# Seven block products for eight in the down-projections and half of the first output projection

## The chip, the cores and the metric

The kernel runs on one core of a Trainium2 chip. The metric is the device time of one execution in microseconds (us). Five engines run their own instruction streams in order: TensorE (PE; its weight loads, PEld, overlap its matmuls), VectorE (DVE), ScalarE (ACT), GpSimd (POOL) and SyncE (SP), which here only issues DMAs. They wait for each other by semaphores.

## What is computed

Two transformer blocks on 256 tokens of width 2048, all in fp32. The first has stick-breaking attention with 16 heads and an MLP with squared ReLU, the second has a mixer of chunked attention and windowed means and a gated MLP with a causal convolution of width 3. Cut to the matrix products that matter here:

```python
# first block
h = x + stick_breaking_mixer(rms_norm(x, norm_mix), w_qkv, w_o)   # ... @ w_o: 2048 x 2048
h = h + jnp.square(relu(rms_norm(h, norm_mlp) @ mlp_w1)) @ mlp_w2 # 2048 x 8192, 8192 x 2048
x = rms_norm(h, final_norm)
# second block
m = concat([attention(q, k, v), pooled], -1) @ w_o_2
x = x + rms_norm(m, post_mix_g)
up = causal_dwconv(rms_norm(x, pre_ffn_g) @ w_up, conv_w, conv_b) # 2048 x 11264
y = (gelu(up[..., :5632]) * up[..., 5632:]) @ w_down              # 5632 x 2048
x = x + rms_norm(y, post_ffn_g)
```

## The kernel before, in words

**Pieces.** Every weight matrix is cut into strips of 512 columns, and a strip into pieces of 256 rows. A piece is one DMA of 512 KB into one of six slots of `raw` (128 partitions, 2 row tiles of 512). `plan_program` writes all 746 pieces and everything around them into one list of steps; each engine's program walks the list and emits what concerns it, so the list is each engine's order. There is no scheduler.

**Three products for one.** An fp32 number is carried as two rounded halves, hi and lo. ACT copies `raw` to `Wh` (L986), DVE makes `Wl = raw - Wh` (L1204), and TensorE computes hi x Wh, hi x Wl and lo x Wh. The tokens are the stationary side, in halves of 128. A piece is 2 token halves x 2 row tiles x 3 = 12 matmuls of 128x512 into the two PSUM banks of one set (`row_products`, all at L1546). Two sets, 0 and 1, take turns from strip to strip; the four banks of set 2 are for side work (scores, turning tiles).

**How far ahead.** `Wh` and `Wl` have `NW = 5` slots. The split of piece i+4 stands in the list just ahead of the products of piece i, and ACT may write it once piece i-1 has been multiplied. So ACT and DVE are never more than four pieces ahead of TensorE. A load of SP waits until the piece six loads earlier has been split.

**Side work around the pieces.** It is put into the same list at a given distance in pieces. Where a strip of `mlp_w1` or `w_up_2` ends, ACT moves the result from PSUM to `T0` (`stage_rows`, L1042 or L1044), SP sends it to DRAM and, three pieces later, reads it back in another order (`land_rows`, L917), and four more pieces later DVE turns 32x32 blocks (`turn_strip`, L1256). For `mlp_w1`, ACT and DVE then split it into `hid1` (L1084, L1325). For `w_up_2`, ACT makes the newest tap of the convolution (L1125, four instructions), DVE the older taps (L1416, eight instructions), ACT the gelu (L1129), POOL the gating product (L1529, 5.5 us), and ACT and DVE split that into `hid2` (L1133, L1422). The row results of `w_o`, `mlp_w2` and `w_down_2` are added on DVE (L1286, L1283, L1440; the first sums of `w_down_2` are copied, L1427), squared and summed on ACT (L998), multiplied by gains on DVE in the last round of the MLP (L1292), and moved over DRAM and turned for the next product (`move_rows` L901 and L906, `turn_blocks` L1296, L1004, L1300).

**The strip pairs.** Output strips of `w_o`, `mlp_w2` and `w_down_2` come in pairs (`strip_pair`). The MLP runs in three rounds (24, 20 and 20 hidden tiles of 128): some strips of `mlp_w1`, then the pair of output columns 0 to 1023, then the pair of 1024 to 2047, over that round's hidden tiles. The gated MLP does the same in two rounds (24 and 20 tiles). I call the two pairs of a round the opening and the second pair.

Of the kernel before, what the change touches and what calls it, by code (L numbers as in the profile page):

```python
# [10 lines left out]
KT = 16  # L11
# [3 lines left out]
NW = 5  # L15
# [37 lines left out]
def plan_program(sem):  # L53
    p = Plan(sem)
    step, done, after, later = p.step, p.done, p.after, p.later
    free = {n: [] for n in ("QK1", "T0", "T1", "E", "zs", "set0", "set1", "set2", "mT", "qk0", "qk1", "v0", "v1", "A0", "A1")}
    st = {}
    now = [0]

    def side_set():  # L60
        return 2
# [60 lines left out]

    def row_squares(n, need, gained=False):
# [6 lines left out]
    def row_norm(squared=False, into=None):  # L130
# [156 lines left out]
    def values(g, blk):  # L287
        def f():
# [4 lines left out]
            free[f"set{s}"] = [lo]  # L293
            oHL_tiles[4 * g:4 * g + 4] = [lo] * 4
# [44 lines left out]
    for s4 in (0, 2):  # L339
        strip_pair("sb_w_o", s4, ALL8, 0 if s4 else 2, "oHL1", oHL_tiles, [evac_rows(s4, "mlp"), evac_rows(s4 + 1, "mlp")])  # L340
# [1445 lines left out]
```

## Time and profile before

| | |
|---|---|
| median of 3 runs | 2097.33 us (2096.52 to 2098.95) |
| profiled execution, its time | 2095.49 us |
| its span (first to last instruction) | 2093.8 us |
| PE busy | 2083.5 us, 9304 matmuls |
| DVE busy | 1224.2 us |
| ACT busy | 1072.2 us |
| granted TensorE clock, mean | 0.999 |
| DMA | 469 MB, mean 224 GB/s |

Start with the busy shares, then ask of each engine what ended its idle time. The share of DVE and ACT is a mean over the program; how far ahead of TensorE they are has to be read place by place in the order of time.

### The profile page before, as it was taken

What the parts mean: (1) busy time and instruction counts of PE and PEld (TensorE: products, weight loads), DVE (VectorE), ACT (ScalarE), POOL (GpSimd) and SP (SyncE); (2) the same over time, 40 slices, a digit from 0 to 9 for tenths busy, and PEclk for the clock granted to TensorE, in tenths of its full rate; (3) what the DMA queues carried; (4) which work ended last, traced back from release to release, by engine and by line L of the source; (5) the groups of instructions that cost most, each with busy time, mean ns of one, the idle gap of its engine ahead of it and who ended that gap; (6) DMA issues with size and microseconds to landing.
All of it is one profiled execution on the core that took longest, in us unless ns stands there. A gap on an engine that the chain in (4) does not pass through costs nothing.

```text
span 2093.8 us, 23749 instructions
## 1 busy us (share of the span) xinstructions
PE 2083.5 (100%) x9304; PEld 1728.1 (83%) x9304; DVE 1224.2 (58%) x1312; ACT 1072.2 (51%) x1303; POOL 119.7 (6%) x66
## 2 busy tenths in 40 slices
PE   9999999999999999999999999999999999999998
PEld 8888888888888888888888888888888888888887
DVE  6546556655554555455566755566666654566665
ACT  7555654555434543455455554455555533555553
POOL 3000000000000000000002000000112100011120
PEclk9999999999999999999999999999999999999999
DMA  8688666888667885688588777667878766787863
GB/s 297 197 251 236 191 188 216 260 248 235 211 193 206 241 254 194 196 243 238 192 270 232 229 244 232 197 203 211 249 236 250 220 211 193 223 247 242 251 221 121
DMA packets 291903, 469.46 MB, mean 224 GB/s; under 512 B 18512, under 2 KB 82128, under 8 KB 291280
## 3 DMA queue, kind: packets, MB, share of 16 engines
q1 hardware_dynamic: 290928, 463.46, 72.5%
q10 hardware_dynamic: 864, 4.49, 0.6%
q8 instruction: 73, 1.20, 0.2%
q14 instruction: 38, 0.31, 0.0%
HBM read 432.75 MB, written 35.13 MB: 223 GB/s over the span
## 4 chain that ended last, share of the span: by engine, by line
PE 96%; DVE 1%; DMA 1%; ACT 1%; issue 0%; SPq 0%; ACTq 0%; DVEq 0%
PE ps L1546 96%; DMA T<-passed_strip 1%; DVE Wl L1204 0%; DVE zs L1416 0%; ACT Wh L986 0%; DMA E<-passed_rows 0%; DVE T L1256 0%; DMA gains<-in_gains_dram 0%; DVE E L1416 0%; ACT zs L1125 0%; SPq L917 0%; DMA passed_rows<-xN 0%; ACT T L1044 0%; DVE aHL L1307 0%; PE ps L1549 0%
## 5 line engine op out<-in xcount | busy, mean ns | idle before, releaser
L1204 DVE TENSOR_TENSOR Wl<-raw,Wh 128x1024 fp32r<-128x1024 f32 x743 | 908.2, 1242 | 674.2 <-ACT Wh L986 673.6
L1546 PE MATMUL ps<-Wh,aHL 128*128 128x512 f32 x3712 | 1148.8, 390 | 2.4 <-DVE Wl L1204 0.8
L986 ACT ACTIVATE Wh<-raw 128x1024 fp32r<-128x1024 f32 x743 | 768.0, 1054 | 611.1 <-PE ps L1546 608.7
L1546 PEld LDWEIGHTS ps<-Wh,aHL 128*128 128x128 f32 x3712 | 696.8, 188 | 147.9 <-DVE Wl L1204 1.3
L1546 PE MATMUL ps<-Wl,aHL 128*128 128x512 f32 x1856 | 722.1, 389 | 0.0
L1546 PE MATMUL ps<-Wh,hid 128*128 128x512 f32 x1728 | 532.8, 389 | 0.0
L1546 PEld LDWEIGHTS ps<-Wl,aHL 128*128 128x128 f32 x1856 | 348.4, 188 | 71.8
L1546 PEld LDWEIGHTS ps<-Wh,hid 128*128 128x128 f32 x1728 | 324.3, 188 | 67.4
L1546 PE MATMUL ps<-Wl,hid 128*128 128x512 f32 x864 | 336.1, 389 | 0.0
L1546 PEld LDWEIGHTS ps<-Wl,hid 128*128 128x128 f32 x864 | 162.2, 188 | 33.7
L1546 PE MATMUL ps<-Wh,oHL 128*128 128x512 f32 x512 | 159.0, 390 | 0.0
L1546 PEld LDWEIGHTS ps<-Wh,oHL 128*128 128x128 f32 x512 | 96.1, 188 | 20.0
L1529 POOL TENSOR_TENSOR E<-E,zs 128x1024 f32<-128x1024 f32 x11 | 60.9, 5534 | 794.8 <-DVE E L1416 794.8
L1546 PE MATMUL ps<-Wl,oHL 128*128 128x512 f32 x256 | 99.6, 389 | 0.0
L1256 DVE STREAM_TRANSPOSE T<-T 128x1024 f32<-128x1024 f32 x38 | 47.2, 1242 | 17.1 <-DMA T<-passed_strip 17.1
L1546 PEld LDWEIGHTS ps<-Wl,oHL 128*128 128x128 f32 x256 | 48.1, 188 | 9.8
L1044 ACT ACTIVATE T<-ps,rs 128x512 f32<-128x512 f32 x72 | 46.0, 676 | 15.6 <-PE ps L1546 7.9
L1520 POOL TENSOR_TENSOR QK<-E 128x1020 f32<-128x1020 f32 x2 | 3.8, 1886 | 821.6 <-DVE E L1256 821.6
L1125 ACT ACTIVATE E<-T,conv 128x256 f32<-128x256 f32 x44 | 22.9, 590 | 44.5 <-DVE T L1256 44.5
L1133 ACT ACTIVATE hid<-E 128x1024 fp32r<-128x1024 f32 x11 | 11.7, 1061 | 65.6 <-POOL E L1529 65.6
L1125 ACT ACTIVATE zs<-T,conv 128x256 f32<-128x256 f32 x44 | 22.9, 590 | 31.9 <-DVE T L1256 31.9
L1084 ACT ACTIVATE hid<-T 128x1024 fp32r<-128x1024 f32 x16 | 17.0, 1062 | 39.2 <-DVE T L1256 39.2
(167 smaller groups left out, 687.4 us busy)
## 6 DMA issues: line engine op xcount, KB each, us to landing
raw<-in_mlp_w_dram SPq DMA_DIRECT2D x256, 512.0 KB, 4.5
raw<-in_w_up_dram SPq DMA_DIRECT2D x176, 512.0 KB, 4.6
raw<-in_sb_w_qkv_dram SPq DMA_DIRECT2D x93, 512.0 KB, 5.2
raw<-in_w_down_dram SPq DMA_DIRECT2D x88, 512.0 KB, 4.7
raw<-in_w_in_dram SPq DMA_DIRECT2D x64, 512.0 KB, 4.8
passed_strip<-T SPq DMA_DIRECT2D x104, 256.0 KB, 4.5
T<-passed_strip SPq DMA_DIRECT2D x208, 128.0 KB, 5.2
raw<-in_sb_w_o_dram SPq DMA_DIRECT2D x32, 512.0 KB, 5.4
```

The lines of the kernel that those rows point to most:

```text
L986: e.activation(Wh[:, i % NW, :], rawv[:, i % NRAW, :], ACT.Copy).then_inc(st["hi"][0], 1)
L1044: e.activation(strip_rows[:, t, :], ps[st["set"]][:, t, :], ACT.Copy, scale=cols[st["col"]][:, t:t + 1]).then_inc(st["staged"][t][0], 1)
L1084: e.activation(hid1[:, st["t0"]:st["t0"] + 4, 0:TOK], T1[:, :, :], ACT.Copy).then_inc(st["hi"][0], 1)
L1125: e.activation(C[:, m, :], T1[:, m, :], ACT.Identity, scale=conv[:, 2, n0 + m:n0 + m + 1], bias=conv[:, 3, n0 + m:n0 + m + 1]).then_inc(st ...
L1133: e.activation(hid2[:, st["t0"]:st["t0"] + 4, 0:TOK], E4, ACT.Copy).then_inc(st["hi"][0], 1)
L1204: e.tensor_tensor(Wl[:, i % NW, :], rawv[:, i % NRAW, :], Wh[:, i % NW, :].bitcast(F32), ALU.subtract).then_inc(st["lo"][0], 1)
L1256: e.transpose(dst, strip_blocks).then_inc(st["done"][0], 1)
L1520: e.tensor_tensor(dst[:, a:4, sh:TOK], src[:, a:4, sh:TOK], src[:, a:4, 0:TOK - sh], ALU.add).then_inc(added[0], 1)
L1529: e.tensor_tensor(E4, E4, Z4, ALU.mult).then_inc(st["done"][0], 1)
L1546: return e.matmul(o, l, r, start=start, stop=stop, skip_group_check=True)
```

## The change

A group of two neighbouring strips x one row pair x two token halves is a 2x2 block product: A (tokens) in four 128x128 blocks, B (weights) in four 128x512 blocks. It takes eight block products of three matmuls before, and seven after, in Winograd's form of Strassen's scheme. 32 groups are done so: two in the second pair of `w_o`, and the first three of each of the ten pairs of `mlp_w2` and `w_down_2`.

- Two pieces become four, s0 to s3, of 6, 6, 6 and 3 matmuls (`seven_products`). s0 and s1 are loaded; the weights of s2, s3 and half of s1 are sums, made by DVE in four additions of 128x512 (`weight_sums`), of which one is in place in `raw`. Each of the four takes a slot of `Wh` and `Wl`, and seven halves of 512 columns are split where four were. `NW` stays 5, and the distances in the list are still counted in pieces.
- The sums of token blocks are made once for each row pair: four DVE instructions, one ACT and one DVE to split them (`mix_tokens`), put behind the hidden tiles or values that they need.
- Four of the seven products collect in the banks of set 2, the others in sets 0 and 1. After the third group (in `w_o` the second), ACT copies one bank and DVE adds the banks into the output rows in eight instructions of 128x512 (`fold`; five in the first round of `w_down_2`, which initialise them).
- In a pair the order is two plain pieces, group, two plain pieces, group, and so on, then the rest. The second strip's PSUM set is now taken by the first group, after two pieces, and not after all plain pieces of the first strip.
- The RMS factor of the MLP is applied under the ReLU (ACT, `scale=`) and no longer squared at the sums, whose scalar_tensor_tensor becomes tensor_tensor; `y_first` adds where it copied.

```diff
+        b[0]["first"], b[0]["start"] = False, (False, True)
+        rest = a[2:n] + b[:n]
+        p.pieces[first:] = a[:2]
+        for m, kp in enumerate(sevens):
+            seven(w, s4, kp, mov, tiles, (a[0]["strip"], b[0]["strip"]), koff, m, m == 0, fold if m == len(sevens) - 1 else None)
+            p.pieces += rest[2 * m:2 * m + 2] if m < len(sevens) - 1 else rest[2 * m:]
+        p.pieces += a[n:] + b[n:]
...
+    def seven(w, s4, kp, mov, tiles, pair, koff, m, opens, fold):
+
+        for i, kind in enumerate(("s0", "s1", "s2", "s3")):
+            src = (w, "rows", kp * 256, (s4 + i) * STRIP) if i < 2 else None
...
+                if t0 < 8:
+                    free["E"] = [lo, mix_tokens("hid2", "E", t0 // 2, 2 if t0 == 0 else 1, [g])]
...
+        if n == 0:
+            made = {m: done("weights_added") for m in (1, 3, 2, 4)}
+            step("weight_sums", a=raw_of[i] % NRAW, b=raw_of[i + 1] % NRAW, need=[landed(i), landed(i + 1), *free["sums"]], made=made)
...
+        step("split", i=i, part=q["kind"], slot=raw_of.get(i, 0) % NRAW, loaded=landed(i) if n == 0 else q["made"],
+             used=(mm_sem, i - NW + 1), hi=(hi_sem, i + 1), lo=(lo_sem, i + 1))
...
+        elif q["kind"] == "s0":
+            if q["opens"]:
+                now[0] = 1 - now[0]
+                set_of[q["pair"][1]] = now[0]
+                need += free[f"set{now[0]}"] + free["set2"]
...
+                elif k == "weight_sums":
...
+                    e.tensor_tensor(wsum[:, 0, :], a[:, 0, :], b[:, 0, :], ALU.add).then_inc(made[1][0], 1)
+                    e.tensor_tensor(b[:, 0, :], b[:, 0, :], b[:, 1, :], ALU.add).then_inc(made[3][0], 1)
+                    e.wait_ge(*made[1])
+                    e.tensor_tensor(wsum[:, 1, :], wsum[:, 0, :], b[:, 1, :], ALU.add).then_inc(made[2][0], 1)
+                    e.wait_ge(*made[2])
+                    e.tensor_tensor(wsum[:, 2, :], wsum[:, 1, :], a[:, 1, :], ALU.add).then_inc(made[4][0], 1)
...
+                elif k == "fold":
...
+                    e.wait_ge(*st["copied"])
+                    e.tensor_tensor(wsum[:, 0, :], P[:, 0, :], wsum[:, 0, :], ALU.add).then_inc(m[0][0], 1)
...
+                    e.tensor_tensor(x[:, 0, a], x[:, 0, a], P[:, 0, :], ALU.add).then_inc(m[1][0], 1)
+                    e.wait_ge(*m[0])
+                    e.tensor_tensor(wsum[:, 1, :], P[:, 2, :], wsum[:, 0, :], ALU.add).then_inc(m[2][0], 1)
+                    e.tensor_tensor(wsum[:, 2, :], P[:, 1, :], wsum[:, 0, :], ALU.subtract).then_inc(m[3][0], 1)
+                    e.wait_ge(*m[2])
+                    e.tensor_tensor(x[:, 1, a], x[:, 1, a], wsum[:, 1, :], ALU.add).then_inc(m[4][0], 1)
+                    e.wait_ge(*m[3])
+                    e.tensor_tensor(wsum[:, 0, :], P[:, 1, :], wsum[:, 1, :], ALU.subtract).then_inc(m[5][0], 1)
+                    e.tensor_tensor(x[:, 0, b], x[:, 0, b], wsum[:, 2, :], ALU.add).then_inc(m[6][0], 1)
+                    e.wait_ge(*m[5])
+                    e.tensor_tensor(x[:, 1, b], x[:, 1, b], wsum[:, 0, :], ALU.add).then_inc(m[7][0], 1)
...
+            def seven_products(q):
...
+                terms = {"s0": (("a11", side[:, 0, :], q["opens"], True), ("a12", a[:, 0, :], False, False)),
+                         "s1": (("d1", side[:, 2, :], q["opens"], True), ("d3", b[:, 0, :], q["opens"], False)),
+                         "s2": (("d0", side[:, 1, :], q["opens"], True), ("d2", side[:, 3, :], q["opens"], True)),
+                         "s3": (("a22", a[:, 1, :], False, False),)}[q["kind"]]
```

**Place 1: DVE in the opening pair of `w_down_2`, first round.** `T1<-T0` is the turning of a strip, `zs` and `E` are the two operands of the gate (128x255 and 128x254 are the older taps), `hid2` is the split of the gated tiles, `Wl` that of a weight piece. Before:

```order
L1204 TENSOR_TENSOR Wl<-raw,Wh 128x1024 [waits s_w_hi] x7
L1256 STREAM_TRANSPOSE T1<-T0 128x1024 [waits s_conv_newest,s_conv_older,s_strip_moved]
L1204 TENSOR_TENSOR Wl<-raw,Wh 128x1024 [waits s_w_hi]
L1416 SCALAR_TENSOR_TENSOR E<-T1,conv,E 128x255 [waits s_conv_newest] x2
L1416 SCALAR_TENSOR_TENSOR E<-T1,conv,E 128x254 [waits s_conv_older] x2
...
L1204 TENSOR_TENSOR Wl<-raw,Wh 128x1024 [waits s_w_hi] x3
L1422 TENSOR_TENSOR hid2<-E,hid2 128x4x256 [waits s_hid_hi]
```

After; `wsum` holds the sums of weights:

```order
L1328 TENSOR_TENSOR Wl<-wsum,Wh 128x1024 [waits s_w_hi]
L1328 TENSOR_TENSOR Wl<-wsum,Wh 128x512 [waits s_w_hi]
L1328 TENSOR_TENSOR Wl<-raw,Wh 128x1024 [waits s_w_hi] x2
L1334 TENSOR_TENSOR wsum<-raw 128x512 [waits s_w_lo,s_raw3,s_raw2]
L1335 TENSOR_TENSOR raw<-raw 128x512
L1337 TENSOR_TENSOR wsum<-wsum,raw 128x512 [waits s_weights_added]
L1339 TENSOR_TENSOR wsum<-wsum,raw 128x512 [waits s_weights_added]
L1328 TENSOR_TENSOR Wl<-raw,Wh 128x1024 [waits s_w_hi] x2
L1328 TENSOR_TENSOR Wl<-wsum,Wh 128x1024 [waits s_w_hi]
L1431 STREAM_TRANSPOSE T1<-T0 128x1024 [waits s_conv_newest,s_conv_older,s_strip_moved]
L1328 TENSOR_TENSOR Wl<-wsum,Wh 128x512 [waits s_w_hi]
```

From the older taps of one strip to the turning of the next stood seven splits for 84 matmuls. Now seven splits for 51 matmuls stand there (s2, s3, two plain pieces, s0, s1, s2: 6 + 3 + 24 + 18), with four additions among them, and behind the turning waits the split of s3, of 3 matmuls.

**Place 2: DVE in the second pair of the last round of `mlp_w2`.** `T1<-E` turns result rows for the next product, `aHL` is their low half. Before:

```order
L1296 STREAM_TRANSPOSE T1<-E 128x1024 [waits s_hid_lo,s_rows_moved]
L1300 SCALAR_TENSOR_TENSOR aHL<-T1,gains,aHL 128x256 [waits s_tile_hi] x4
L1204 TENSOR_TENSOR Wl<-raw,Wh 128x1024 [waits s_w_hi] x4
L1296 STREAM_TRANSPOSE T1<-E 128x1024 [waits s_tile_lo,s_rows_moved]
L1300 SCALAR_TENSOR_TENSOR aHL<-T1,gains,aHL 128x256 [waits s_tile_hi] x4
L1204 TENSOR_TENSOR Wl<-raw,Wh 128x1024 [waits s_w_hi] x3
```

After:

```order
L1467 STREAM_TRANSPOSE T1<-E 128x1024 [waits s_hid_lo,s_rows_moved]
L1471 SCALAR_TENSOR_TENSOR aHL<-T1,gains,aHL 128x256 [waits s_tile_hi] x4
L1328 TENSOR_TENSOR Wl<-raw,Wh 128x1024 [waits s_w_hi]
L1334 TENSOR_TENSOR wsum<-raw 128x512 [waits s_w_lo,s_raw5,s_raw4]
L1335 TENSOR_TENSOR raw<-raw 128x512
L1337 TENSOR_TENSOR wsum<-wsum,raw 128x512 [waits s_weights_added]
L1339 TENSOR_TENSOR wsum<-wsum,raw 128x512 [waits s_weights_added]
L1328 TENSOR_TENSOR Wl<-raw,Wh 128x1024 [waits s_w_hi] x2
L1328 TENSOR_TENSOR Wl<-wsum,Wh 128x1024 [waits s_w_hi]
L1467 STREAM_TRANSPOSE T1<-E 128x1024 [waits s_tile_lo,s_rows_moved]
L1471 SCALAR_TENSOR_TENSOR aHL<-T1,gains,aHL 128x256 [waits s_tile_hi] x4
L1328 TENSOR_TENSOR Wl<-wsum,Wh 128x512 [waits s_w_hi]
```

Between the two turnings stood four splits for 48 matmuls; now there are four splits for 30 (12 + 6 + 6 + 6) and four additions.

## Rows read from the trace of the kernel before

**Rows 1.** The page: span, and busy us of each engine with its share

```profile
span 2093.8 us, 23749 instructions
...
PE 2083.5 (100%) x9304; PEld 1728.1 (83%) x9304; DVE 1224.2 (58%) x1312; ACT 1072.2 (51%) x1303; POOL 119.7 (6%) x66
```

**Rows 2.** TensorE's waits: us in total, times, longest us

```profile
PE ps L1546 <- ACT zs L1149: 2.3, 1, 2.3
```

**Rows 3.** Windows: length, PE, PEld, DVE, ACT, POOL busy (x), granted clock, DMA share, GB/s

```profile
500.00:700.00 200.00, 200.00 (x884) 165.62 (x883) 101.89 (x88) 86.36 (x89) 0.00 (x0) 1.00 0.70 212
2086.00:2093.00 7.00, 1.41 (x3) 0.30 (x2) 3.77 (x10) 1.93 (x5) 0.00 (x0) 0.83 0.51 185
```

**Rows 4.** The timeline of TensorE from 600 us: start us, us, what

```profile
600.41 0.62 PE L1546 MATMUL ps<-Wh,hid 128*128 128x512 f32 x2
...
601.09 0.62 PE L1546 MATMUL ps<-Wh,hid 128*128 128x512 f32 x2
```

**Rows 5.** The timeline of DVE in a plain stretch; idle time before, and its releaser

```profile
529.23 1.23 DVE L1204 TENSOR_TENSOR Wl<-raw,Wh 128x1024 fp32r<-128x1024 f32 x1 [1.50 <-ACT Wh L986]
```

**Rows 6.** Groups by line: busy us, mean ns of one, idle before

```profile
L1204 DVE TENSOR_TENSOR Wl<-raw,Wh 128x1024 fp32r<-128x1024 f32 x743 | 908.2, 1242 | 674.2 <-ACT Wh L986 673.6
...
L1286 DVE TENSOR_TENSOR xN<-xN,ps 128x512 f32<-128x512 f32 x8 | 5.1, 681 | 0.0
...
L986 ACT ACTIVATE Wh<-raw 128x1024 fp32r<-128x1024 f32 x743 | 768.0, 1054 | 611.1 <-PE ps L1546 608.7 <-DMA raw<-in_sb_w_qkv_dram 2.0
```

**Rows 7.** The timeline of DVE, opening pair of w_down_2, first round

```profile
1620.98 1.22 DVE L1422 TENSOR_TENSOR hid<-E,hid 128x1024 fp32r<-128x1024 f32 x1 [3.38 <-ACT hid L1133]
1622.12 4.62 DVE L1204 TENSOR_TENSOR Wl<-raw,Wh 128x1024 fp32r<-128x1024 f32 x4
1626.66 1.24 DVE L1256 STREAM_TRANSPOSE T<-T 128x1024 f32<-128x1024 f32 x1
1630.99 1.23 DVE L1204 TENSOR_TENSOR Wl<-raw,Wh 128x1024 fp32r<-128x1024 f32 x1 [3.09 <-ACT Wh L986]
1632.13 3.25 DVE L1416 SCALAR_TENSOR_TENSOR zs<-T,conv,zs 128x255 f32<-128x255 f32 x8
...
1650.06 1.25 DVE L1256 STREAM_TRANSPOSE T<-T 128x1024 f32<-128x1024 f32 x1 [2.86 <-DMA T<-passed_strip]
1654.41 1.22 DVE L1204 TENSOR_TENSOR Wl<-raw,Wh 128x1024 fp32r<-128x1024 f32 x1 [3.10 <-ACT Wh L986]
```

**Rows 8.** The timeline of ACT there

```profile
1627.93 2.08 ACT L1125 ACTIVATE zs<-T,conv 128x256 f32<-128x256 f32 x4 [3.20 <-DVE T L1256]
1629.91 1.04 ACT L986 ACTIVATE Wh<-raw 128x1024 fp32r<-128x1024 f32 x1
1630.86 1.24 ACT L1044 ACTIVATE T<-ps,rs 128x512 f32<-128x512 f32 x2
```

**Rows 9.** The timeline of SP there: the strip's way back from DRAM

```profile
1640.26 1.97 SPq L917 DMA_DIRECT2D T<-passed_strip  x4
```

**Rows 10.** Matmuls on hidden tiles after 1500 us: ns min/median/max, first and last start

```profile
L1546 PE MATMUL ps<-Wh,hid x704: 389/389/389, 1628.3 to 2085.0; 128*128 128x512 f32 x176
```

**Rows 11.** The timeline of DVE, second round's opening pair

```profile
1968.41 3.49 DVE L1204 TENSOR_TENSOR Wl<-raw,Wh 128x1024 fp32r<-128x1024 f32 x3
...
1973.76 1.25 DVE L1256 STREAM_TRANSPOSE T<-T 128x1024 f32<-128x1024 f32 x1 [0.16 <-DMA T<-passed_strip]
```

**Rows 12.** The timeline of DVE around the last round's second pair of mlp_w2

```profile
1019.97 1.40 DVE L1283 SCALAR_TENSOR_TENSOR xN<-ps,rs,xN 128x512 f32<-128x512 f32 x2
...
1038.19 1.24 DVE L1296 STREAM_TRANSPOSE T<-E 128x1024 f32<-128x1024 f32 x1
1040.01 1.69 DVE L1300 SCALAR_TENSOR_TENSOR aHL<-T,gains,aHL 128x256 fp32r<-128x256 f32 x4 [0.58 <-ACT aHL L1004]
...
1049.51 1.25 DVE L1296 STREAM_TRANSPOSE T<-E 128x1024 f32<-128x1024 f32 x1 [2.72 <-DMA E<-passed_rows]
```

**Rows 13.** The timeline of DVE at the second turning in w_o's pairs

```profile
358.94 1.25 DVE L1296 STREAM_TRANSPOSE T<-E 128x1024 f32<-128x1024 f32 x1 [2.57 <-DMA E<-passed_rows]
```

More of the change, by code:

```diff
@@ L55, in plan_program @@
     step, done, after, later = p.step, p.done, p.after, p.later
-    free = {n: [] for n in ("QK1", "T0", "T1", "E", "zs", "set0", "set1", "set2", "mT", "qk0", "qk1", "v0", "v1", "A0", "A1")}
+    free = {n: [] for n in ("QK1", "T0", "T1", "E", "zs", "set0", "set1", "set2", "mT", "qk0", "qk1", "v0", "v1", "A0", "A1", "sums")}
     st = {}
     now = [0]
+    taken = []
     def side_set():
+        assert not taken
         return 2
@@ L90, in strip, with strip_pair @@
             p.pieces.append(dict(src=src, shape=2, mov=mov, kt=2 * (kp - koff), tiles=tiles, kind="N", first=n == 0,
-                                 last=n == len(ks) - 1, evac=evac, early=None, strip=strips[0]))
+                                 start=(n == 0, n == 0), last=n == len(ks) - 1, evac=evac, early=None, strip=strips[0]))
         return first
-    def strip_pair(w, s4, ks, tail, mov, tiles, evacs, koff=0):
-        first, n = len(p.pieces), len(ks) - tail
+    def strip_pair(w, s4, ks, tail, mov, tiles, evacs, koff=0, sevens=(), fold=None):
+        plain = [kp for kp in ks if kp not in sevens]
+        first, n = len(p.pieces), len(plain) - tail
@@ new lines, in strip_pair @@
+        b[0]["first"], b[0]["start"] = False, (False, True)
[5 more added lines that the diff above has]
+        p.pieces += a[n:] + b[n:]
+        order = [q["strip"] if q["kind"] == "N" else 0 for q in p.pieces[first:]]
@@ new lines, in strip_pair @@
+        assert max(j for j, k in enumerate(order) if k == 0) < max(j for j, k in enumerate(order) if k == a[0]["strip"])
+        assert min(j for j, k in enumerate(order) if k == 0) < min(j for j, k in enumerate(order) if k == b[0]["strip"])
+        return first
+    def seven(w, s4, kp, mov, tiles, pair, koff, m, opens, fold):
+        for i, kind in enumerate(("s0", "s1", "s2", "s3")):
+            src = (w, "rows", kp * 256, (s4 + i) * STRIP) if i < 2 else None
+            p.pieces.append(dict(src=src, shape=2, mov=mov, kt=2 * (kp - koff), tiles=tiles, kind=kind, m=m, first=False,
+                                 opens=opens, last=False, evac=None, early=None, strip=None, pair=pair,
+                                 fold=fold if i == 3 else None, closes=fold is not None))
@@ L293, in f @@
             free[f"set{s}"] = [lo]
+            if blk == 1 and g == 0:
+                free[f"set{s}"] = [lo, mix_tokens("oHL1", "values", 0, 2, [lo])]
             oHL_tiles[4 * g:4 * g + 4] = [lo] * 4
@@ L617, in f @@
                 d = [done("y_kept") for t in range(2)]
-                step("y_first", s4=s4, set=s, mm=k, done=d)
+                step("y_first", s4=s4, set=s, mm=k, folded=st.pop(("fold", s4)), done=d)
                 free[f"set{s}"] = [d[1]]
@@ L681, in split @@
             load_x_rest(i)
-            load(i + NRAW)
+            load(raw_of[i] + NRAW)
+        elif i < N and p.pieces[i]["kind"][0] == "s":
+            sums_and_split(i)
         elif i < N:
-            step("split", i=i, loaded=(raw[i % NRAW], 16 * (i // NRAW + 1)), used=(mm_sem, i - NW + 1) if i >= NW else None,
+            step("split", i=i, part="N", slot=raw_of[i] % NRAW, loaded=landed(i), used=(mm_sem, i - NW + 1) if i >= NW else None,
                  hi=(hi_sem, i + 1), lo=(lo_sem, i + 1))
             load_x_rest(i)
-            load(i + NRAW)
+            load(raw_of[i] + NRAW)
     x_rows = []
@@ L741, in plan_program @@
                 need.append(tok)
-        q["set"], q["n"] = 2 if q["kind"] == "P" else set_of[q["strip"]], i
+        q["n"] = i
+        q["set"] = 2 if q["kind"] == "P" else [set_of[n] for n in q["pair"]] if q["kind"][0] == "s" else set_of[q["strip"]]
         if i < N - HELD:
@@ L759, in plan_program @@
             q["evac"](q["set"], k)
+        if q.get("fold"):
+            taken.clear()
+            q["fold"](q["set"], k)
         for job in p.later_steps.pop(i, ()):
```

209 lines of the change are left out of this document (160 added, 49 removed).

## The prediction

> **What bounds the kernel now.** The page first: PE is busy in 2083.5 of 2093.8 us, DVE in 58% and ACT in 51% [rows 1]. Then PE's own waits, to see whether it ever stands: the longest is 2.3 us, at the very end [rows 2]. So TensorE sets the time and each matmul taken away is worth its pitch. The timeline of TensorE gives it: three matmuls, one block product, start every 601.09 - 600.41 = 0.68 us [rows 4], at a granted clock of 1.00, which is the 2.4 GHz level, in the window of 500 to 700 us [rows 3]. A plain piece lasts 2.72 us.
>
> The second thing to see is by how much the splits are early, since the change takes from exactly this. In a plain stretch DVE waits 1.50 us for ACT ahead of each split [rows 5]: a piece's slot is free when TensorE begins the piece four places earlier, ACT's hi takes 1.05 us, DVE's lo 1.23, and with the waits the piece is ready about 2.6 us after that start, 10.9 - 2.6 = 8.3 us early. This lead is the cover of everything DVE and ACT do besides.
>
> **What is taken away.** 32 groups x one block product = 96 matmuls: 32 x 0.68 = **21.8 us**. All on the path.
>
> **What is added, in a stretch where nothing else happens.** A group and the two plain pieces behind it: TensorE 7 x 0.68 + 5.44 = 10.2 us. DVE: five splits of 1024 at 1.14 us (four in a row took 4.62 from start to end, the last one's tail included [rows 7]), half a split, 0.65, and four additions of 512. A 512-wide tensor_tensor takes 0.68 and, back to back, 5.1/8 = 0.64 [rows 6]; one addition waits for the one before it, so 2.6 for four. Sum 8.95 of 10.2 us. ACT needs 5.5 x 1.05 = 5.8. So the scheme holds by itself, but only by 1.25 us in 10.2, and the lead is smaller: four places ahead are now s1, s2, s3 and a plain piece, say, and not 48 matmuls. Worked through place by place, s0 is ready some 2.7 us ahead of its use, and a plain piece behind s3 some 2.4 us. Anything above 2.5 us that DVE has to do, or to wait for, inside the groups makes TensorE stand. The fold (8 additions, about 5.4 us, once per pair) does not: four plain pieces, 10.9 us, are split ahead of it, and the next split is ready about 1 us early. The tokens' sums in the strips of `mlp_w1` cost DVE and ACT about 4 us against the full lead: nothing. The new scale under the ReLU and the changed row sums: within 0.1 us each, nothing.
>
> On 512-wide additions the Trainium skill (VectorE: DVE Perf Modes, The TRN2 errata) says that each instruction pays a fixed time, and gives an fp32 tensor_tensor (N+151)/0.96 ns. That makes 0.69 us for 512; the trace agrees, 0.68 alone [rows 6], but back to back the fixed part is mostly hidden (0.64 and 1.14), so four additions priced by the page would be 2.8 and not 2.6 us.
>
> **Opening pair of w_down_2, first round** (place 1 of the change). The pair's first matmul starts at 1628.3 [rows 10]. With unchanged times up to there, s0 is due at 1628.3 + 5.4 = 1633.7, s1 at 1635.1, s2 at 1636.4, s3 at 1637.8. DVE: the four splits from 1622.12 become three, to 1625.5 [rows 7]; additions to 1628.3; lo of s0 to 1629.5; the turning, 1.24, to 1630.7; ACT's four taps of 2.08 in all [rows 8] to 1632.8; ACT's hi of s1 to 1633.9, then the two copies to `T0`, 1.24 together, to 1635.1, which free the PSUM set that the group now needs at once (due 1633.7), hi of s2 to 1636.1. DVE: lo of s1 to 1635.1, eight older taps, 3.2 [rows 7], to 1638.2, lo of s2 to 1639.4. TensorE stands about 3 us by then, and 0.6 more for the plain piece behind s3, since ACT's gelu stands ahead of its hi. The next strip's way back from DRAM: SP issues it behind a load that waits for that plain piece's split, at 1642.1; in the trace the turning starts 9.8 us after the issue at 1640.26, having waited for it [rows 7, 9]; so 1651.9. Before that, DVE has the splits up to the next group's s2 ready, and s3 is due at 1651.6. But turning 1.25, taps on ACT 2.1, hi and lo of s3 1.3: 1656.5, **4.9 us late**. Then 3.2 of older taps and the split of a plain piece, due 0.7 after s3 began: **3.6 us late**. Last, the gate's split (POOL 5.6 us, then ACT and DVE, which waits: 3.38 us before [rows 7]) stands between s0 and s1 of the third group: 1.0. Sum **13 us**. Before, the same block, 9.8 us from the turning to the end of the second split, met about 8 us of pieces already split and 2.7 us of the one between.
>
> **Second round's opening pair.** The same order, DVE a little earlier against TensorE: three splits are done at 1971.9 [rows 11], 4.6 us ahead of the pair's start, and not 2.8. That spares 2.5 of the first 3.6 us: **10 us**.
>
> **Second pair of the last MLP round** (place 2). DVE adds rows, ACT squares them, DVE multiplies them by gains, ACT squares again, each ahead of a split; one turning with its four low halves takes 1038.19 to 1041.7, 3.5 us, and a split follows 0.5 later [rows 12]. Against TensorE, with the pair's times from 1020.2: s3 of the first group is ready 16.6 after that and due at 15.0 (1.6 late), the plain pieces behind it 0.8 and, behind the turning, 2.5 late, s0 of the next group 1.1; the second turning waits for its rows until about 30 (before: to 1049.51, with a wait of 2.72 [rows 12]), so the s3 behind it is 3 late. Sum **9.5 us**.
>
> **Second pair of w_o.** The same without gains and squares: 0.6 behind the first turning; the second waits for its rows (2.57 before [rows 13]), and s2 and s1's lead are used up: 5. Sum **5.5 us**.
>
> **The rest.** Opening pairs of `mlp_w2`: a turning, ACT's and DVE's halves, 3.6 us, between s2 and s3 against a lead of 2.9 and 0.4 behind it: 1 us each, 3. The tokens' sums of `hid2` stand behind the gate's split, where the lead had already shrunk to about 2.2 us (the split that starts at 1622.12 is due at 1625.6 [rows 7, 10]): 4.1 and 2.6 us of work, 2.3 us per round, 4.6. The sums of `oHL1` the same way, 0 to 2, taken as 1. The other six second pairs and the program's end: nothing.
>
> Sum of the stalls: 13 + 10 + 9.5 + 5.5 + 3 + 4.6 + 1 = **46.6 us** against 21.8. On the profiled execution (2095.5 us) that is +24.8, 2120.3; the median lies 1.8 us above it, so **2122 us**. From below the stalls are bounded by what waits for nothing outside DVE and ACT: the block of turning, taps and hi and lo alone, without DRAM's delay, by a rough estimate 60% of the sum, 28 us; from above by DMA landings later by 1 to 2 us at six turnings, 60 us.
>
> **Rivals.**
> - *The lead is better than I make it, and TensorE hardly stands.* For it: means of 58% and 51% [rows 1]; DVE would rise only to about 69%. DVE's idle time in front of ACT is large. Against it: the row-by-row order above. It needs all stalls under 17 us. At 10 us of stalls: 2097.3 - 21.8 + 10 = 2086 us. This one ends faster; it decides at the turning between s2 and s3, if that costs under 2 us and not 8.5. Chance 0.14.
> - *Stalls and saving about cancel*: DVE's backlog is eaten by its own idle gaps, 17 to 28 us of stalls: 2093 to 2103, middle 2098. Chance 0.14.
> - *The clock falls in the stalls.* In the trace's last 7 us, where TensorE stood 2.3 us and more, the granted clock was 0.83 in the mean, between 1.2 and 2.4 GHz [rows 2, 3]; nowhere before had it stood as long. Some five stalls here are of 3.5 to 5 us. If each brings the clock down and one plain piece after it runs at half rate, that is 5 x 2.7 = 13.5 us more, 2136. Against it: after most of the stalls DVE is the later one, and slower matmuls hide in its time. Chance 0.12. The Trainium skill (TensorE: Matmul & The Clock Gate, HAM oscillation) states this rule, that a TensorE standing too long restarts at half clock; no row here shows it in the middle of a kernel.
> - *The forecast*, 2103 to 2133. Chance 0.60.
>
> **The numbers.** Low end 2090 (leaves out most of the first rival), high end 2138 (takes in the clock). Faster and slower are counted from 0.2%, 4.2 us, about what a measurement of this kernel can tell. Faster: the first rival, 0.14. Same, 2093 to 2101.5: half of the second and a little, 0.08. Slower: 0.78.
>
> **What would show it.** In the profile after: 9208 matmuls and a pitch of still 0.68 per three; PE's waits on DVE's splits of 40 to 50 us in all, where before they were 0.8; the longest of 4 to 5 us at the s3 behind a turning in both opening pairs of `w_down_2`; DVE near 69%; the plain strips as long as before. Wrong: if PE's waits on DVE stay under 15 us, the lead was misjudged; if the pitch of the group's matmuls is not 0.227 us each, the saving was.

## The result, and the profile after

The changed kernel takes **2136.18 us** (median of 4 runs, 2134.44 to 2138.98), against 2096.93 (2095.73 to 2098.95) for the kernel before beside it: a ratio of 1.0187, 95% interval 1.0170 to 1.0205. It is slower by 39 us where I forecast 25. The profiled execution took 2138.98 us, the most of the four; so the stages below, read from the profiles, account for 43 us and not for 39. Its page, busy us and share of each engine [rows 1]:

```profile
span 2136.7 us, 24135 instructions
...
PE 2086.4 (98%) x9208; PEld 1718.6 (80%) x9208; DVE 1428.4 (67%) x1640; ACT 1136.3 (53%) x1390; POOL 121.9 (6%) x66
```

There are 96 matmuls fewer, as there should be, and PE is busy for 2.9 us longer: part of them ran slowly, as shown below. TensorE's waits [rows 2]; columns: us in total, times, longest:

```profile
PE ps L1719 <- DVE Wl L1328: 31.9, 23, 3.3
PE ps L1719 <- ACT T L1167: 3.7, 2, 2.6
PE ps L1722 <- DVE xN L1463: 3.4, 1, 3.4
PE ps L1719 <- DVE aHL L1471: 2.6, 1, 2.6
```

The first line is the splits. The second is the PSUM set that a group needs at once and that ACT still has to copy. The third and fourth are no weights at all: rows of the next stage's input that come late.

To see where the time went I measured each stage from the start of its first matmul to that of the next stage's (the last row: to the start of the last matmul on weights). Us, from the starts in both traces; "forecast" is the time before, less the saving, plus the prediction's stalls:

| stage | before | forecast | after |
|---|---|---|---|
| `w_o`, second pair | 43.5 | 47.6 | 45.9 |
| `mlp_w1`, first round | 130.6 | 130.6 | **135.0** |
| three opening pairs of `mlp_w2` | 174.1 | 171.0 | 170.6 |
| second pairs of `mlp_w2`, rounds 1 and 2, and of `w_down_2`, round 1 | 185.0 | 178.9 | 178.8 |
| second pair of `mlp_w2`, round 3 | 54.4 | 61.9 | 61.6 |
| `w_in_2` | 188.4 | 188.4 | **193.6** |
| `w_up_2`, both rounds | 483.0 | 487.6 | **494.3** |
| opening pair of `w_down_2`, round 1 | 65.3 | 76.2 | 76.5 |
| the same, round 2 | 54.4 | 62.4 | 64.4 |
| second pair of `w_down_2`, round 2 | 54.2 | 52.1 | **54.3** |

The pairs themselves came out nearly as worked through in their sums. For the profiled execution I forecast 2120.3 us, 18.7 too few. 16.3 of them lie in other stages, in bold; with the last pair's 2.2 nearly all are found.

**The opening pair of `w_down_2`**, DVE in the first round [rows 7]; start us, us, engine, line, op, tiles, idle time before and its releaser:

```profile
1649.99 1.24 DVE L1431 STREAM_TRANSPOSE T<-T 128x1024 f32<-128x1024 f32 x1
1654.32 1.23 DVE L1328 TENSOR_TENSOR Wl<-raw,Wh 128x1024 fp32r<-128x1024 f32 x1 [3.09 <-ACT Wh L1100]
1655.46 3.24 DVE L1587 SCALAR_TENSOR_TENSOR zs<-T,conv,zs 128x255 f32<-128x255 f32 x8
...
1668.37 1.22 DVE L1328 TENSOR_TENSOR Wl<-wsum,Wh 128x1024 fp32r<-128x1024 f32 x1
1669.54 1.25 DVE L1431 STREAM_TRANSPOSE T<-T 128x1024 f32<-128x1024 f32 x1
1673.44 0.69 DVE L1328 TENSOR_TENSOR Wl<-wsum,Wh 128x512 fp32r<-128x512 f32 x1 [2.66 <-ACT Wh L1100]
1674.05 3.24 DVE L1587 SCALAR_TENSOR_TENSOR E<-T,conv,E 128x255 f32<-128x255 f32 x8
1677.21 2.36 DVE L1328 TENSOR_TENSOR Wl<-raw,Wh 128x1024 fp32r<-128x1024 f32 x2
```

The second turning starts behind a split and finds its rows there, the split of s3 comes 3.9 us later, then the older taps, then the plain piece. SP had issued the rows' way back [rows 9] here:

```profile
1662.97 1.95 SPq L1025 DMA_DIRECT2D T<-passed_strip  x4
```

TensorE there [rows 4]:

```profile
1674.19 0.50 PE L1719 MATMUL ps<-Wh,hid 128*128 128x512 f32 x1 [1.80 <-DVE Wl L1328]
1674.53 0.40 PE L1719 MATMUL ps<-Wl,hid 128*128 128x512 f32 x1
1674.76 0.40 PE L1719 MATMUL ps<-Wh,hid 128*128 128x512 f32 x1
1678.48 0.80 PE L1719 MATMUL ps<-Wh,hid 128*128 128x512 f32 x1 [3.32 <-DVE Wl L1328]
1679.08 0.63 PE L1719 MATMUL ps<-Wl,hid 128*128 128x512 f32 x1
1679.50 1.05 PE L1719 MATMUL ps<-Wh,hid 128*128 128x512 f32 x2
```

Three matmuls of s3, and TensorE stands for 3.32 us. Then it goes on at half its rate: 1679.08 to 1679.50 is 0.42 us from start to start, where 0.23 was normal. Windows of these moments [rows 3]; length, PE, PEld, DVE, ACT, POOL busy, granted clock, DMA share, GB/s:

```profile
1647.30:1688.00 40.70, 32.63 (x123) 25.01 (x122) 34.07 (x45) 21.34 (x29) 6.24 (x1) 0.87 0.55 172
400.00:412.00 12.00, 9.40 (x35) 7.32 (x34) 7.04 (x14) 7.12 (x11) 0.00 (x0) 0.86 0.69 218
1460.00:1472.00 12.00, 9.93 (x37) 7.77 (x36) 8.44 (x10) 6.23 (x8) 0.00 (x0) 0.86 0.65 186
```

By such starts there are eight slow stretches of four matmuls or more, 67 matmuls in all with 13.9 us more than at the full rate; before there was none. DVE is busy in 34.1 of the pair's first 40.7 us, and waits for ACT in most of the rest.

**The first strips of `mlp_w1`** show a stall that I had not looked for. DVE adds the result rows of `w_o`'s second pair (L1457) and turns them (L1467); before, the same are L1286 and L1296. Before:

```profile
365.19 1.28 DVE L1286 TENSOR_TENSOR xN<-xN,ps 128x512 f32<-128x512 f32 x2
...
384.18 1.28 DVE L1286 TENSOR_TENSOR xN<-xN,ps 128x512 f32<-128x512 f32 x2
...
396.20 1.25 DVE L1296 STREAM_TRANSPOSE T<-E 128x1024 f32<-128x1024 f32 x1 [4.47 <-DMA E<-passed_rows]
```

After:

```profile
375.17 1.28 DVE L1457 TENSOR_TENSOR xN<-xN,ps 128x512 f32<-128x512 f32 x2
...
386.18 1.25 DVE L1467 STREAM_TRANSPOSE T<-E 128x1024 f32<-128x1024 f32 x1 [3.28 <-DMA E<-passed_rows]
...
392.44 1.28 DVE L1457 TENSOR_TENSOR xN<-xN,ps 128x512 f32<-128x512 f32 x2
...
403.32 1.25 DVE L1467 STREAM_TRANSPOSE T<-E 128x1024 f32<-128x1024 f32 x1 [4.29 <-DMA E<-passed_rows]
```

The pair starts at 340.2 before and 341.2 after, `mlp_w1` at 383.7 and 387.0. The groups stand among the pieces of the pair's *first* strip, so that its rows are added 34.0 us after the pair's start and not 25.0. Its turning then falls just ahead of the second strip's rows: these are added 5.4 us after `mlp_w1` began, and not 0.5, and turned 16.3 us after, not 12.5. TensorE is there first:

```profile
406.13 0.67 PE L1719 MATMUL ps<-Wh,aHL 128*128 128x512 f32 x1 [2.60 <-DVE aHL L1471]
```

**`w_up_2`**: DVE where the first tokens' sums of `hid2` stand:

```profile
1460.89 1.23 DVE L1593 TENSOR_TENSOR hid<-E,hid 128x1024 fp32r<-128x1024 f32 x1 [3.38 <-ACT hid L1256]
...
1463.16 0.42 DVE L1354 TENSOR_TENSOR wsum<-wsum,E 128x256 f32<-128x256 f32 x1
1464.71 1.22 DVE L1356 TENSOR_TENSOR hidMix<-wsum,hidMix 128x1024 fp32r<-128x1024 f32 x1 [1.13 <-ACT hidMix L1108]
1465.85 3.49 DVE L1328 TENSOR_TENSOR Wl<-raw,Wh 128x1024 fp32r<-128x1024 f32 x3
```

From the end of the gate's split, 1462.1, to the start of the next weight's at 1465.85 are 3.7 us, and TensorE stood for 2.1 us until 1467.2. The second sums, 46 us later, take only 2.7 us and made it stand for 2.2.

### The profile page after: what moved, and what is told of

Its sections match the earlier page's. It is cut to its first block and busy times, and to the rows that moved or that the text cites. A ratio compares the mean times of both kernels' runs of the same rounds, so it can differ in the third digit from the quotient of the medians.

```text
span 2136.7 us, 24135 instructions
## 1 busy us (share of the span) xinstructions
PE 2086.4 (98%) x9208; PEld 1718.6 (80%) x9208; DVE 1428.4 (67%) x1640; ACT 1136.3 (53%) x1390; POOL 121.9 (6%) x66
## 5 line engine op out<-in xcount | busy, mean ns | idle before, releaser
L1719 PE MATMUL ps<-Wh,hid 128*128 128x512 f32 x1428 | 455.3, 395 | 23.7 <-DVE Wl L1328 19.9
L1719 PEld LDWEIGHTS ps<-Wh,hid 128*128 128x128 f32 x1428 | 271.6, 190 | 88.3 <-DVE Wl L1328 27.2
L1719 PE MATMUL ps<-Wl,hid 128*128 128x512 f32 x714 | 280.8, 393 | 0.0
L1719 PEld LDWEIGHTS ps<-Wl,hid 128*128 128x128 f32 x714 | 135.9, 190 | 27.9
L1719 PE MATMUL ps<-Wh,hidMix 128*128 128x512 f32 x240 | 79.5, 392 | 1.4 <-DVE Wl L1328 1.4
L1328 DVE TENSOR_TENSOR Wl<-wsum,Wh 128x1024 fp32r<-128x1024 f32 x64 | 60.1, 963 | 21.7 <-ACT Wh L1100 21.6
L1100 ACT ACTIVATE Wh<-wsum 128x1024 fp32r<-128x1024 f32 x64 | 52.2, 834 | 13.8 <-PE ps L1719 13.8
L1719 PEld LDWEIGHTS ps<-Wh,hidMix 128*128 128x128 f32 x240 | 45.3, 189 | 11.9 <-DVE Wl L1328 2.4
```

Source lines behind the costliest of these rows:

```text
L1100: e.activation(Wh[:, i % NW, c], src, ACT.Copy).then_inc(st["hi"][0], 1)
L1328: e.tensor_tensor(Wl[:, i % NW, c], src, Wh[:, i % NW, c].bitcast(F32), ALU.subtract).then_inc(st["lo"][0], 1)
L1719: return e.matmul(o, l, r, start=start, stop=stop, skip_group_check=True)
```

## The experiments

Times are compared with the kernel before on the same chip (2094.9 to 2095.5 us there). The edits are given in short form; the kernels name the pairs that have groups in one table. A stage's time is that of the one profiled execution.

**The crowded places plain.**

```diff
-                   sevens=(0, 1) if s4 else (), fold=fold_into("xN", s4, lambda: [x_rows[-1]]))
+                   sevens=(), fold=fold_into("xN", s4, lambda: [x_rows[-1]]))
...
-                           sevens=tuple(range(2 * at, 2 * at + 3)), fold=...
+                           sevens=() if c == 2 and s4 == 2 else tuple(...), fold=...    # mlp_w2
+                           sevens=() if s4 == 0 else tuple(...), fold=...               # w_down_2
```

> The changed kernel without the groups of seven at the four places where a turning stands among them: second pair of w_o, last second pair of mlp_w2, both opening pairs of w_down_2 (21 of 32 groups stay; all token sums are still made). Theory, the lead is used up only there: the two w_down_2 pairs come back from 76.5 and 64.4 us to 65.3 and 54.4, the mlp_w2 pair from 61.6 to 54.4, the w_o pair from 45.9 to 43.5, and the starts of mlp_w1 and w_in_2 behind two of them (4.4 and 5.2 us longer) as well; in all about 40 us less, 2096. Rival, the load of DVE as such makes TensorE stand, wherever it is: a third less of it brings a third of the lost time back, 2120 or so.

Measured: 2101.33 us (2096.64 to 2105.23, 10 runs), ratio 1.0025 [1.0016, 1.0035]: the theory, some 5 us above its number. `mlp_w1` took 131.1 us, `w_in_2` 188.4 and the last round's second pair of `mlp_w2` 54.9. So 35 of the 41 us hang on 11 of the 32 groups, and what `mlp_w1` and `w_in_2` take longer goes with the groups in the pair ahead of them. What stays lies mostly in `w_up_2` (+5.2 and +3.8) and in the openings, which were 1.6 and 2.9 above before without a group of their own.

**Weight sums of two columns.**

```diff
-    e.tensor_tensor(wsum[:, 0, :], a[:, 0, :], b[:, 0, :], ALU.add)
+    e.tensor_tensor(wsum[:, 0, 0:2], a[:, 0, 0:2], b[:, 0, 0:2], ALU.add)   # and so the other three
```

> The changed kernel with the four additions of each weight sum cut from 512 columns to 2, all waits kept; the products of the sums are not the right ones. It takes some 1.8 us of DVE out of each group, 58 us in all. Theory (place and lead, a chain of turning, ACT and split): opening pairs of w_down_2 stay over 70 and 59 us, since the chain behind the turning stays; in all 2112 to 2122. Rival (DVE's load): every pair comes down to two us under its old time, in all 2085 to 2095.

The other 510 columns of each sum hold old values. Measured: 2137.11 us, one run. Neither theory gives this time, and only the openings are as the first said. DVE was busy for 61.5 us less (1366.9, 64% of the span), and TensorE waited for its splits as long as before, 32.1 us. The openings of `w_down_2` fell by 2.8 and 3.3 us, to 73.7 and 61.1, for some 5 us of DVE's time spared in each; the opening pair of `mlp_w2` in round 2 rose by 4.0, to 58.2, `mlp_w1` in the first round to 136.4, `w_in_2` to 195.3. DVE's mean load is not what holds TensorE up; what the losses elsewhere came from is open.

**Later.** Tokens' sums of `hid2` eight pieces later in both rounds, and ten plain pieces ahead of the first group in the first round's opening of `w_down_2`; the second round's opening keeps its order.

```diff
-    p.pieces[first:] = a[:2]
+    p.pieces[first:] = (a[:n] + b[:n])[:at]          # at = 10 in that pair, 2 in all others
...
-    free["E"] = [lo, mix_tokens("hid2", "E", t0 // 2, 2 if t0 == 0 else 1, [g])]
+    later(8, mix)                                     # the same call
```

> Two edits at two places. In the first round's opening pair of w_down_2 the first group comes after ten plain pieces and not after two, the same work in another order; and the token sums of hid2 are made eight pieces later, in both rounds. Theory: that pair goes from 76.5 us to 64 or 66; w_up_2 strips from 272.0 and 222.3 to 267 and 219; in all 2136 - 11 - 8 = 2117. Rival (DVE's load): the same instructions, so the same time, 2136 give or take 3.

Measured: 2122.33 us (2117.61 to 2124.10, 4 runs), ratio 1.0131 [1.0114, 1.0148]. The profiled execution is the fastest of the four, 2117.61. The rival falls; of the theory, the strips of `w_up_2` did better than said and are back at exactly 265.4 and 217.6 us, but the first round's opening took 69.4 and not 64 to 66, with three stalls of 2.3, 2.5 and 0.9 us left in it. The second round's took 62.3, 2.1 less, though its groups were not moved. DVE in `w_up_2`, with the gate's split at the same place as above and no sums behind it:

```profile
1460.97 1.23 DVE L1600 TENSOR_TENSOR hid<-E,hid 128x1024 fp32r<-128x1024 f32 x1 [3.37 <-ACT hid L1263]
1462.11 3.49 DVE L1335 TENSOR_TENSOR Wl<-raw,Wh 128x1024 fp32r<-128x1024 f32 x3
```

**Tokens' sums alone**, no groups at all, so that nobody reads them.

```diff
-    sevens=...        # at all eleven places
+    sevens=()
```

> No groups of seven at all, but all token sums are still made (and the RMS factor sits under the ReLU). It prices the token sums by themselves. Theory: the strips of w_up_2 are 4 to 7 us longer per round than before, the attention's 1 us, everything else as before: 2105 to 2109. Rival: those strips were longer for another reason, then 2097 to 2099.

Measured: 2108.69 us, one run: the theory, at its upper end. `w_up_2` took 273.2 and 222.0 us, +7.8 and +4.4, every other stage what it took before within 0.3. With the run above this settles the part of `w_up_2`: 11 to 12 us, all from the place of these sums.

**No standing, no slow clock.**

```diff
+    if st["i"] in EXTRA:          # seven pieces, 9 to 14 each, ahead of the piece's waits
+        for n in range(EXTRA[st["i"]]):
+            mm(own[:, 0, 0:128], spare[:, 0:128], spare[:, 128:256], False, False)
```

> The changed kernel, and ahead of seven pieces at which TensorE stood for 2.2 to 3.5 us it multiplies a tile of zeros into the running sums, 9 to 14 small matmuls of 128 columns, for about as long as it would have waited. Nothing that ACT, DVE or a DMA does is changed. In the changed kernel the matmuls behind these seven places started at half their rate, 8 to 13 of them each, and 13.0 us were lost in them. Theory A (the standing brings the clock down, and the time is lost for good): the stretches run at the full rate and the time falls from 2136 to 2123 to 2127 us. Theory B (DVE is the later one behind a stall, so slower matmuls hide in its time, as the prediction argued against its third rival): the granted clock is better, the waits for DVE grow by the same amount, and the time stays at 2133 to 2138 us.

Measured: 2136.95 us, one run, mean granted clock 0.997 for 0.991. Slow stretches: three for eight, 4.3 us for 13.9; two of the three are new ones, at other matmuls. The place shown above, now (one small matmul shows as two records):

```profile
1671.12 3.29 PE L1732 MATMUL ps<-spare 128*128 128x128 f32 x28
1674.60 0.50 PE L1732 MATMUL ps<-Wh,hid 128*128 128x512 f32 x1 [0.20 <-DVE Wl L1335]
...
1681.57 0.47 PE L1732 MATMUL ps<-Wh,hid 128*128 128x512 f32 x1 [1.23 <-DVE Wl L1335]
...
1683.75 0.50 PE L1732 MATMUL ps<-Wh,hidMix 128*128 128x512 f32 x1 [0.55 <-DVE Wl L1335]
```

The granted clock in the pair's window is 1.00 where it was 0.87:

```profile
1647.00:1690.00 43.00, 38.81 (x193) 31.74 (x192) 36.12 (x46) 25.91 (x33) 6.24 (x1) 1.00 0.52 162
```

At full rate TensorE is through the two plain pieces earlier and waits 1.23 and 0.55 us for s0 and s1 of the third group, two stalls that the changed kernel did not have there. By its time this is theory B: the slow matmuls mostly ran in time that DVE needed anyway. It is not all hidden: `mlp_w1` gained 1.9 us, the first opening 2.2, `w_up_2` 1.3 in round 1, but later stages lost about as much (0.9 to 1.4 each in the last round's second pair of `mlp_w2`, `w_in_2`, `w_up_2` and the opening of round 2). One run can't separate that from the scatter of the changed kernel's runs, 4.5 us. In three of the seven places the small matmuls left no wait at all, so they may have held TensorE up a little themselves; that was not tried apart. A gain of 13 us did not come.

**One plain piece more ahead of the groups.**

```diff
-    p.pieces[first:] = a[:2]
+    p.pieces[first:] = (a[:n] + b[:n])[:at]          # at = 3 in the two openings of w_down_2, 2 in all others
```

> The changed kernel with one more plain piece ahead of the first group in the two opening pairs of w_down_2 (three for two), so that the turning stands ahead of the split of s2 and not of s3. Same work on every engine, same DMAs. Theory A (what decides is how many matmuls are queued ahead of the split behind the turning and of the one behind the older taps: 36 and 42 for the second turning, where it is 30 and 33 now): the two waits of 2.0 and 3.5 us behind it shrink by 1.4 and 2.0, the first round's opening pair takes 72 to 74 us and not 76.5, the time is 2129 to 2133. Theory B (the mean load of DVE in the pair, or the landing of the turned rows, decides): 76 to 77 us and 2135 to 2138.

Measured: 2142.36 us, one run; the openings took 77.2 and 66.3 us. Neither theory, and theory A, which counts matmuls ahead of a split, misses its range by 9 us. DVE in the first round:

```profile
1670.46 1.24 DVE L1436 STREAM_TRANSPOSE T<-T 128x1024 f32<-128x1024 f32 x1
1674.79 1.23 DVE L1333 TENSOR_TENSOR Wl<-wsum,Wh 128x1024 fp32r<-128x1024 f32 x1 [3.09 <-ACT Wh L1105]
...
1685.43 1.23 DVE L1598 TENSOR_TENSOR hid<-E,hid 128x1024 fp32r<-128x1024 f32 x1 [3.38 <-ACT hid L1261]
1686.57 0.69 DVE L1339 TENSOR_TENSOR wsum<-raw 128x512 f32<-128x512 f32 x1
```

The two stalls behind the turning were 2.0 and 3.5 us and are 2.8 and 1.2: 1.5 less together, where 3.4 were expected; the first group's wait for its PSUM set, 2.7 us, is gone as well, with two of 0.4 and 0.7 in its place. But the gate's split now stands with its 3.38 us of waiting right ahead of the additions, and s0 of the third group kept TensorE waiting 3.9 us, with 14 slow matmuls behind. Here a stall that was moved past one block met the next.

**The side work of the openings made thin.** The taps, gelu and gating product of the last strips are cut to 8 columns, so that part of the gated tiles is stale.

```diff
-    e.activation(C[:, m, :], T1[:, m, :], ACT.Identity, ...
+    w = slice(0, 8) if st["j"] in (5, 10) else slice(0, TOK)
+    e.activation(C[:, m, w], T1[:, m, w], ACT.Identity, ...     # and so the older taps, gelu and gate
```

> The changed kernel; for the last strip of each half in each round of w_up_2 (the two whose turning stands in an opening pair of w_down_2) the taps, the gelu and the gating product work on 8 columns for 256, so that part of the gated tiles is left as it was. The turnings, the way over DRAM, all groups, additions and splits stay. Theory A (what stands between the groups is the cause: the turning's block of 9.8 us would lose 1.2 us of ACT's and 2 us of DVE's taps, and nothing waits for POOL): the first round's opening pair 67 to 70 us for 76.5, the second's 57 to 60 for 64.4, the time 2121 to 2127. Theory B (the splits and additions of the groups themselves, with the turnings' delay over DRAM, hold TensorE up): over 73 and 62 us, 2131 to 2137.

Measured: 2123.48 us, one run; the openings took 68.9 and 58.8 us, for 76.5 and 64.4. Theory A, in all three numbers. TensorE's stalls in the first opening were 1.9, 1.6 and 1.4 us, with no slow stretch. The second turning's block:

```profile
1666.33 1.25 DVE L1439 STREAM_TRANSPOSE T<-T 128x1024 f32<-128x1024 f32 x1 [0.97 <-DMA T<-passed_strip]
1669.41 0.69 DVE L1336 TENSOR_TENSOR Wl<-wsum,Wh 128x512 fp32r<-128x512 f32 x1 [1.83 <-ACT Wh L1106]
1670.02 1.17 DVE L1596 SCALAR_TENSOR_TENSOR E<-T,conv,E 128x7 f32<-128x7 f32 x8
```

**Groups only where nothing is turned among them.**

```diff
+GROUPS = {("mlp", 0, 0): 2, ("mlp", 1, 0): 2, ("mlp", 2, 0): 2, ("mlp", 0, 2): 2, ("mlp", 1, 2): 2, ("down", 0, 2): 2}
...
+    later(8, mix)            # tokens' sums of hid2; those of oHL1 and of round 2 are gone
```

> Groups of seven only in six pairs: the three opening and the first two second pairs of mlp_w2, and the second pair of w_down_2 in its first round; 18 groups. w_o, the last round's second pair of mlp_w2 and the other three pairs of w_down_2 are plain, the sums of tokens that nobody reads are left out, and those of hid2 stand eight pieces later. Theory A (the saving is real wherever nothing is turned between the groups, 2.0 us in a second pair and 0.2 to 1.7 in an opening one): 1.7 + 2.1 + 0.4 + 2.0 + 1.6 + 2.1 = 9.9 less, 0.5 to 2 more elsewhere: 2087 to 2090 us, ratio 0.996. Theory B (the additions cost as much elsewhere, through later turnings and loads, as they save): 2094 to 2099 us.

Measured: 2089.16 us (2084.28 to 2090.66, 5 runs), ratio **0.9966** [0.9953, 0.9978]. Theory A.

**The last pair too.** The same kernel, with `("down", 1, 2): 2` added to the table and the sums of `hid2` that this pair needs.

> The kernel of the six pairs, and groups in the very last pair too (the second of w_down_2, second round; its 3 groups and their token sums, eight pieces later). In the changed kernel this pair took 54.3 us for 54.2 before, though it has 6.1... 2.0 us less to multiply. Theory A (its stall is its own, next to the end): no gain, 2087 to 2091 us, within 1 us of the six pairs. Theory B (its stall came from the late opening pair ahead of it, which is plain here): 2.0 us less than the six pairs, 2085 to 2088 us.

Measured: 2086.76 us (2084.86 to 2087.84, 5 runs), ratio **0.9956** [0.9942, 0.9969]: faster than both kernels. It lies 2.4 us below the six pairs, which by the time alone is theory B; yet the gain isn't in the pair, which again took 54.3 us behind a plain opening pair. The profiled execution was ahead by 3.0 us before that pair began, mostly in the openings, which are the same in both. So its stall is its own, as theory A says of the pair, and the 2.4 us are scatter or something that is not known; the runs of the two kernels overlap. Its profile, busy times and TensorE's waits:

```profile
PE 2073.7 (99%) x9241; PEld 1717.4 (82%) x9241; DVE 1357.4 (65%) x1540; ACT 1116.2 (54%) x1362; POOL 119.2 (6%) x66
...
PE ps L1731 <- DVE Wl L1335: 3.2, 5, 1.9
```

21 groups are worth 21 x 0.68 = 14.3 us; 7.7 arrived in the span (2093.8 to 2086.1). These are the same seven pairs as in the first experiment, 2101.33 us: what differs is that the tokens' sums of `hid2` stand eight pieces later and those that nobody reads are left out. Between them lie 14.6 us, 9.9 of them in `w_up_2` and 3.3 in the openings of `w_down_2`. So the places of the groups brought 35 us, and the places of the tokens' sums decided between a loss of 0.25% and a gain of 0.4%. DVE at 65% is hardly less loaded than in the changed kernel at 67%, and TensorE waits for its splits 3.2 us and not 31.9.

## Why the forecast was right and wrong

- **The time.** 2122 forecast, 2136.18 measured: 14 us off, and outside my own band of 2103 to 2133. It lies inside 2090 to 2138 only because the high end took in the rival of the clock, whose price the run with the gaps filled does not bear out. That much is luck; the direction is not.
- **What bounds the kernel, the saving.** Right. 32 block products went, and where nothing stands among the groups a pair lost 2.0 to 2.1 us, as it should (three second pairs: 178.8 us, forecast 178.9).
- **The lead, counted in matmuls and not in pieces.** Right in what it says of the places: thin side work gave back 7.6 and 5.6 us of the openings, groups in places without turnings pay, and 61.5 us less of DVE's busy time changed nothing. As a count it is not confirmed: the run that tested it, one plain piece more ahead of the groups, came out 9 us above its range.
- **Opening pairs of `w_down_2`.** 13 and 10 us; measured 13.3 and 12.0, but with another division: in the first round 2.7 us at s0 (forecast about 3 at the set and the taps), 0.5 at the plain piece behind the first s3 (0.6), 2.0 at the next s3 (4.9), 3.5 at the plain piece behind it (3.6), nothing at the gate (1.0). That is 8.7 of waits for 13, and slow matmuls made up the rest; that the sums agree is partly luck. The 4.9 was mis-sized by the landing of the turned rows: before, the last of the four transfers had landed 9.8 us after the first was issued, and I took this over [rows 7, 9]; now it was 6.5, issued 15.7 us into the pair and landed just as DVE came to the turning, at 22.2.
- **Second pair of the last MLP round.** 9.5; measured 7.2 + 2.0 = 9.2. **Second pair of `w_o`**: 5.5; measured 3.7, mainly one stall of 2.8 at s2 of the second group (the turned rows were in time). **Openings of `mlp_w2`**: 3; measured 2.6.
- **"The other six second pairs and the program's end: nothing."** Wrong for the last second pair: 2.2 us. The fold's additions and the strip's rows stand on DVE ahead of a split, and TensorE waited 1.89 us for it until 2117.2 in the changed kernel, and until 2066.6 in the one with seven pairs.
- **The sums of `hid2`, 4.6 us.** Mechanism right, size wrong: 11.2. Forecast 1.9 us for the first sums of a round and 0.4 for the second. Measured 2.1 and 2.2 in the first round, none and 2.2 in the second: the lead of 2.2 us, read at one gate's split, did not hold at the others. Two stretches of half-rate matmuls behind these stalls, 1.6 and 1.5 us, came on top. The sums of `oHL1`, taken as 1: the first stage was 1.2 us longer, but only 0.3 with the tokens' sums alone, so this can't be told from scatter.
- **What I left out**, the main fault of the working: 4.4 us in `mlp_w1` and 5.2 in `w_in_2`, terms that the sum had at nothing. The working followed each pair to its end and took the next stage as unchanged. In `mlp_w1` 2.8 us are the stall shown above and 1.6 the slow matmuls behind it. The rows of `w_o`'s first strip come 9 us later, and the turnings shift into the next stage. That this comes from the groups in these pairs is shown (131.1 and 188.4 without them); that it comes through the first strip's rows is read from the timelines and was not tried by itself.
- **The rivals.** "The lead is better" and "cancel" fell: TensorE's waits for splits were 31.9 us. "The clock falls in the stalls" came true as an event, in eight places and not five, and its time, 2136, is the one measured. The slow matmuls even add up to its price, 13.9 us for 13.5. But, as far as one run shows, this was not the kernel's loss: with seven of the eight gaps filled the time stayed. By places the miss is 4.4 + 5.2 + 6.6 + 2.2 us, where I had nothing or too little. As the prediction argued against this rival, DVE was mostly the later one. Of the Trainium skill's rule (TensorE: Matmul & The Clock Gate, HAM oscillation) the trace now shows the event in the middle of a kernel, 0.86 and 0.87 in the windows above, but not after every stand: two of 2.6 and 2.2 us, until 363.1 and 1512.5, had no slow stretch behind them.
- **What would show it.** DVE at 67% (69 said), pitch unchanged, waits for splits 31.9 (40 to 50 said), the longest 3.3 and behind s3, not at it (4 to 5 said).

## What to carry to other kernels

When a change makes TensorE faster and feeds it with more work of DVE, measure DVE's lead in time at every place where it also waits for something, and put the new work where nothing of this kind stands; here 21 groups of 32, with the tokens' sums moved out of the way too, gained 0.4% and all 32 lost 1.9%, at nearly the same mean load. Small helper work counts as much as the main one: the same 21 groups with the sums where they were still lost 0.25%. Follow each delayed result into the next stage too: half of what the forecast missed was in stages that the change does not touch. In the one run that tried it, a stall moved by one piece met the next block; moving by eight or ten pieces helped.

## What the hardware showed

- TensorE at half rate (start to start 0.42 us for 0.23, the 1.2 GHz level for 2.4) behind eight stands of 2.1 to 3.4 us in the middle of the kernel, for 4 to 13 matmuls each, and not behind two others of 2.2 and 2.6 us; yet with seven of the eight filled, three stages gained 5.4 us together and the time of the kernel stayed.
- In both openings of `w_down_2` one addition of 128x512 on DVE took four times its 0.69 us, while POOL made the gating product of 128x1024, which itself took 6.2 us both times, where the nine others took 5.1 to 5.6. A split and three additions under the same product kept their usual times. The same addition took 0.69 where POOL's product had 8 columns. Both times it was the fourth addition of the third group; why only that one was not tried.

```profile
1680.68 0.69 DVE L1337 TENSOR_TENSOR wsum<-wsum,raw 128x512 f32<-128x512 f32 x1
1681.40 2.76 DVE L1339 TENSOR_TENSOR wsum<-wsum,raw 128x512 f32<-128x512 f32 x1
...
1677.37 6.24 POOL L1702 TENSOR_TENSOR E<-E,zs 128x1024 f32<-128x1024 f32 x1 [36.73 <-DVE E L1587]
```
